# Moving the start of the first output projection's weight work on GpSimd ahead, into the last attention head

## The reference, cut to what matters

```
s = einsum('bqhd,bkhd->bhqk', qb, k) * scale;  s = where(causal, s, -inf)
pr = softmax(s);  out = einsum('bhqk,bkhd->bqhd', pr, v)
ym = mla_branch(...) * silu(gm)
mix = concatenate([ys, ym], axis=-1) @ w_out[i]
u = DEEPNORM_ALPHA * x + mix
ple = sigmoid(u @ w_pg[i]) * (p[i] @ w_pp[i])
```

```
ada = silu(c) @ w_ada[i] + b_ada[i]
```

## Time and profile before

| | |
|---|---|
| time, median of 3 runs | 2152.24 us (2151.87 to 2154.48) |
| the profiled execution's own time | 2153.62 us |
| its span in the profile | 2151.8 us |
| PE busy | 2074.0 us (96% of the span) |
| POOL busy | 1140.8 us (53%) |
| chain that ended last | PE 80%, DVE 8%, POOL 3%, ACT 3% |
| mean granted TensorE clock | 0.989 of full speed |

### The profile page before, as it was taken

One profiled execution on the slowest core, in us unless ns is written; L12 is line 12 of the kernel. 1 busy time (PEld: TensorE's weight loads), 2 busy tenths in 40 slices (PEclk: granted clock), 3 DMA queues, 4 the chain that ended last, 5 costly groups with the idle time before them and its releaser, 6 DMA issues.

```text
span 2151.8 us, 28447 instructions
## 1 busy us (share of the span) xinstructions
PE 2074.0 (96%) x11124; PEld 1629.0 (76%) x11124; DVE 1359.5 (63%) x1705; ACT 817.9 (38%) x1304; POOL 1140.8 (53%) x793
## 2 busy tenths in 40 slices
PE   8999999989998999999999999998999999999997
PEld 5878746978866885578757788876788888877885
DVE  7999865631967115510168325775977777778988
ACT  6232243330126006610174443145554554453443
POOL 2576713067872754337656664474787777850000
PEclk9999999999999999999999999999999999999998
DMA  7463461052224120101221235233122222247543
GB/s 302 146 144 108 115 173 63 1 205 92 89 90 140 60 98 28 28 30 69 57 48 56 82 118 205 88 118 137 50 80 73 83 89 88 69 159 256 186 139 112
DMA packets 72725, 230.02 MB, mean 107 GB/s; under 512 B 15959, under 2 KB 18823, under 8 KB 71279
## 3 DMA queue, kind: packets, MB, share of 16 engines
q1 hardware_dynamic: 59632, 170.04, 23.3%
q10 hardware_dynamic: 9104, 36.45, 4.6%
q0 software_dynamic: 3856, 21.70, 3.9%
HBM read 180.03 MB, written 46.17 MB: 105 GB/s over the span
## 4 chain that ended last, share of the span: by engine, by line
PE 80%; DVE 8%; POOL 3%; ACT 3%; issue 2%; DMA 2%; SPq 1%; ACTq 0%; DVEq 0%; POOLq 0%
PE ps L3563 22%; PE ps L3160 18%; PE ps L3678 8%; PE ps L3487 4%; PE ps L3596 4%; PE ps L3182 3%; PE ps L3634 2%; DVE back L2350 2%; PE ps L355 2%; PE ps L3125 1%; PE ps L525 1%; PE ps L513 1%; PE ps L378 1%; PE ps L507 1%; PE ps L538 1%
## 5 line engine op out<-in xcount | busy, mean ns | idle before, releaser
L1779 POOL TENSOR_TENSOR up_parts<-front,up_parts 128x512 fp32r<-128x512 f32 x120 | 188.6, 1581 | 74.6 <-ACT up_parts L2087 73.9
L3678 PE MATMUL ps<-ffn_parts,w_parts 128*128 128x512 f32 x924 | 214.5, 394 | 5.5 <-DVE ffn_parts L2946 5.4
L3678 PEld LDWEIGHTS ps<-ffn_parts,w_parts 128*128 128x128 f32 x924 | 175.3, 190 | 44.1 <-DVE w_parts L2938 3.8
L3563 PE MATMUL ps<-t_high,up_parts 128*128 128x512 f32 x640 | 204.1, 390 | 1.0 <-ACT back L2094 0.8
L3160 PE MATMUL ps<-h_high,w_parts 128*128 128x512 f32 x672 | 187.6, 394 | 0.6 <-PE ps L3487 0.6
L1704 POOL TENSOR_TENSOR w_parts<-front,sb_zero 128x1024 fp32r<-128x1024 f32 x48 | 100.4, 2091 | 161.9 <-PE ps L3487 61.7
L3563 PE MATMUL ps<-h_high,up_parts 128*128 128x512 f32 x480 | 154.9, 389 | 0.3 <-DVE back L2755 0.2
L1709 POOL TENSOR_TENSOR w_parts<-front,w_parts 128x1024 fp32r<-128x1024 f32 x54 | 142.9, 2647 | 19.3 <-ACT w_parts L2252 6.3
L3160 PEld LDWEIGHTS ps<-h_high,w_parts 128*128 128x128 f32 x672 | 124.0, 188 | 25.8 <-issue 1.4
L3563 PEld LDWEIGHTS ps<-t_high,up_parts 128*128 128x128 f32 x640 | 120.1, 188 | 27.1 <-issue 1.4
L1590 POOL TENSOR_TENSOR front<-front,sb_csilu 128x1024 f32<-128x1024 f32 x48 | 102.9, 2144 | 58.8 <-DMA front<-w_ada 58.7
(11 more groups left out here) (445 smaller groups left out, 5029.2 us busy)
## 6 DMA issues: line engine op xcount, KB each, us to landing
front<-w_ada SPq DMA_DIRECT2D x48, 512.0 KB, 3.5
front<-w_up SPq DMA_DIRECT2D x44, 512.0 KB, 4.2
front<-w_down SPq DMA_DIRECT2D x22, 512.0 KB, 3.6
back<-w_down SPq DMA_DIRECT2D x22, 512.0 KB, 4.4
front<-w_in SPq DMA_DIRECT2D x16, 512.0 KB, 4.2
front<-w_out SPq DMA_DIRECT2D x16, 512.0 KB, 4.4
residual<-back ACTq DMA_DIRECT2D x2, 4096.0 KB, 14.7
front<-w_gates SPq DMA_DIRECT2D x16, 512.0 KB, 4.3
```

The costliest lines, as they stand in the source:

```text
L1779: pool.tensor_tensor(parts[:, BANK:], src, parts[:, 0:BANK].bitcast(F32), ALU.subtract)\
L3563: mm = pe.matmul(o, parts[:, at + k * P:at + (k + 1) * P], x, start=p in (1, 2, 5) and k == 0 and q == 0, stop=k == 3 and q == 2, skip_gro ...
L3678: mm = pe.matmul(ps[:, (4 if p in (2, 5, 3) else 0) + m, :], weights[:, w_ * BANK + m * P:w_ * BANK + (m + 1) * P], half_of(x, x_), start= ...
```

## The change

GpSimd makes part of its work for the output projection earlier in its program: the parts of output block 0, modulation sum 16, the rounded part of block 1, and modulation sum 17 now stand ahead of the load of `XN`, behind a wait for the scores of the last head's first query block (`mla_scores_read` of 27: 25 score tiles and 2 turned heads). The low part of block 1 follows behind the load of `XN`. The loop over the blocks starts at 2, and the load of `PP`, which was issued behind block 0's parts, is issued behind block 2's.

```diff
+            def first_high(j):
+                b = B_WOUT + 2 * j
+                pool.wait_ge(S(f"w_landed{b % RING}"), 16 * (b // RING + 1))
+                pool.tensor_tensor(w_parts_1(b)[0], ring[:, b % RING, :], zero[:, 0:1].to_broadcast((P, PAGE)), ALU.add)\
+                    .then_inc(S("w_high"), 1)
+            def first_low(j):
+                b = B_WOUT + 2 * j
+                pool.wait_ge(S("w_high"), j + 1)
+                pool.tensor_tensor(w_parts_1(b)[1], ring[:, b % RING, :], w_parts_1(b)[0].bitcast(F32), ALU.subtract)\
+                    .then_inc(S("w_split"), 1)
+            pool.wait_ge(S("mla_scores_read"), 8 * (MLA_HEADS - 1) + MLA_HEADS - 1)
+            first_high(0)
+            first_low(0)
+            ada_sum(16)
+            first_high(1)
+            ada_sum(17)
             pool.wait_ge(S("mla_turned"), 32)
             pool.dma_start(XN, xn_dram).then_inc(S("xn_back"), 16)
...
-            for j in range(8):
+            first_low(1)
+            for j in range(2, 8):
                 split(B_WOUT + 2 * j)
-                if j == 0:
+                if j == 2:
                     pool.dma_start(PP, pp_dram.rearrange("a p k t -> p a k t")).then_inc(S("pp_back"), 16)
                 ada_sum(16 + j)
```

## The result

The changed kernel takes 2156.7 us in the median of 22 runs (2152.9 to 2163.5), the kernel before 2153.5 in 22; the ratio is 1.0017 with an interval of 1.0011 to 1.0024. It is slower by 0.17%, 3.7 us (2.4 to 5.2), where 2.2 less was forecast. One run of the kernel before took 2603 us and is not part of the comparison. The profiled execution took 2154.1 us with a span of 2152.3.

What follows compares the result with a forecast made beforehand. PE, busy for 96% of the span, was taken to bound the kernel, so only its waits could be won: -4.2 for earlier products + 2.0 for a new stall = -2.2, and 2152.24 - 2.2 = 2150.0 us, range 2147.8 to 2152.9.

Steps and rivals of the forecast that it cites:

- The two waits: PE's waits for GpSimd's low parts ahead of products 0 and 1 of the output projection, 3.7 us together, would go.
- the gain: Products 0 and 1 start earlier without their waits: 1.86, 2.19 and 0.11 us, sum 4.2, at least 3.7.
- GpSimd's work did not slow the last head: Moved GpSimd work beside the attention's last head priced at nothing; the slower rival said 2159.1 us, chance 0.04.
- the 1.3 us kept for them: Possible loss in product 0 if DVE's four low parts took 2.06 us each; not priced, kept for the range.
- the new wait: PE waits ahead of product 3 for GpSimd's low part, held up by modulation block 18's load, about 2 us.
- The allowed 7.5 us: Time modulation block 18's load may take before product 3 is late; every microsecond more stalls PE.
- that is about 9.5 and a stall of 2.0: Modulation block 18's load beside PP's takes about 9.5 us, so PE stalls 2.0 ahead of product 3.
- about 1 for queueing: Part of the time of modulation block 18's load: about 1 us for queueing behind packets already taken.
- the 85 used: Rate in GB/s of SP's queue beside PP's load, giving 6.2 us for modulation block 18's 0.52 MB.
- The row of 12.0: Output block 2's load beside XN and PP took 12.0 us, not 3.5; used as upper case, stall 4.5.
- the sum of rates: Duration of modulation block 18's load: 6.2 us at 85 GB/s, 2.4 for start and landing, about 1 for queueing.
- The meeting costs the whole: Rival: modulation block 18's load takes 12.0 us or more beside PP's, stall 4.5, time 2152.5 to 2153.9; chance 0.15.

Runs made afterwards that it cites:

- the repeat: The changed kernel run once more, unedited, timed against the kernel before: ratio 1.0011 (1.0002 to 1.0020).
- the first experiments: Follow-up runs timed beside the kernel before, not listed singly; the first one told moved PP's load right behind XN's in the changed kernel: ratio 0.9974.
- the run from ScalarE's queue: The changed kernel with PP's load issued from ScalarE's queue behind the sixth bias piece, at 462.80 us: ratio 1.0016 (1.0007 to 1.0025) to the kernel before.
- the kernel before with the collision: The kernel before, nothing made ahead, with PP's load moved to just ahead of block 2's parts: ratio 1.003 (1.002 to 1.0039).

## Why the prediction was wrong

**Right.** The two waits went, and the gain was 4.2 to 4.3: SP's issue of block 18 came 21.86 behind the turning before (467.95 - 446.09) and 17.58 after (463.28 - 445.70). GpSimd's work did not slow the last head: 640-wide tiles read 23.99 apart there (416.13 to 440.12), as between the heads before (392.14 to 416.13). DVE's four low parts took 4.63 instead of the 8.24 of the earlier trace rows, 1.16 each instead of 2.06, while GpSimd stood idle (446.4 to 458.1); so the 1.3 us kept for them were not needed, and XN's chain was in time. The place of the new wait, its cause, PP's issue (462.4 where 462.6 was forecast) and the load's (463.3 where 463.65 was) came out as written. The allowed 7.5 us were right too: 12.1 - 7.5 = 4.6, measured 4.4.

**Wrong, first: the duration of the load in PP's company.** The wait ahead of product 3 was 4.4, where the prediction had about 2 and called itself wrong above 4. The step "that is about 9.5 and a stall of 2.0" is the one that failed, and in it the "about 1 for queueing". In the changed kernel SP's queue moved its first packets between 467.2 and 467.4, about 4 us behind the issue at 463.28, where alone (the load at 467.95 in the kernel before) it had them about 1 us behind; so the start costs some 3 more, not 1. By 474 the queue had moved 0.52 MB, in 6.8 us at 77 GB/s, near the 85 used and the 6.2 that came of them. So 2 of the missing 2.6 us are the start and 0.6 the rate. The late start stood already in the trace of the kernel before: the load that took 12.0 was issued at 448.79, and SP's queue is absent from the view of 450 to 452 us (first row) and has 16 packets in that of 452 to 454 (second row), over 3 us behind the issue:

```profile
q0 software_dynamic: 24, 0.79, 91.0%
...
q1 hardware_dynamic: 16, 0.07, 8.0%
```

The row of 12.0 was the better guide than the sum of rates: it was set aside because XN's packets are larger, and that made no difference to the total. "The meeting costs the whole" was the rival that came true.

**Wrong, second: a term that no case had.** The prediction looked for the price of a stall only in PE's waiting. Behind a stall of 4.4 us the clock stood at half for 3.5 us, and half a product took 1.8 us longer. With it the sum is -4.3 + 4.4 + 1.8 = +1.9, and the trace has nearly that, 2.0: the column of product 3 ended 44.08 behind the turning before (490.17 - 446.09), and 46.11 after (491.81 - 445.70). The same 2.0 still stands in later products (616.53 - 446.09 before, 618.17 - 445.70 after), and half of it goes in the norm that follows (653.29 - 446.09 before, 653.88 - 445.70 after), where the granted clock was 0.81 over 630 to 665 us against 0.76; the span ends 0.5 longer. That the clock made this difference is likely, not shown.

**Open.** The 22 runs say 3.7 (2.4 to 5.2), the repeat 2.4 (0.4 to 4.3), the trace 2.0. The mean granted clock over the 22 runs was 0.9880, in 33 runs of the kernel before (those beside the first experiments) 0.9894, so the changed kernel seems to spend more time at half clock than its profiled executions show. The 8.24 of the run from ScalarE's queue, where the other traces have 7.3 to 7.4, is one way in which that can come about. How often it does, no trace shows.

The range ended at 2152.9, since it held the rival's cost without what follows a stall. With both terms the sum would be -4.2 + 4.5 + 1.8 = +2.1, still a little under the 2.4 at which the interval of the 22 runs begins. And 1.2 of the distance from 2150.0 to 2156.7 is the starting point: the kernel before has a median of 2153.5 in 22 runs, and had 2152.24 in the three that the forecast went by.

## What to carry to other kernels

When work is made earlier, list every DMA issue that moves with it, and see which small load that the critical engine depends on is issued within the next microseconds: a load of 4 MB with 16 KB packets turned one of 0.5 MB from 3.5 into 12 us. Put the large one where the small ones have slack, or cut it so that its packets are as short. Price a stall of TensorE of some 4 us above its length, for the clock behind it (here 1.8 to 2.7 more, restart included); and where the trace has one row of the disputed wait, take it before a figure built from rates. Here the early start is worth 0.26% (0.16 to 0.36) with PP's load moved up, and was -0.17% without.

## What the runs showed that was not expected

- Two queues on the same DMA engines got equal numbers of packets, not of bytes: 41 to 39 with 0.67 to 0.16 MB, and 114 to 116 with 0.43 to 0.41 MB. The Trainium skill ("DMA: Bandwidth & Descriptors", section "Queues, rings and completion order") has this rule, and the trace agrees, if the packets of the profile are taken as those of the Trainium skill; the same from SP and ScalarE (38 to 40) as from SP and GpSimd.
- A load issued behind another starts late: first packets about 4 us behind the issue with 16 KB packets ahead and 3 with 4 KB packets, against about 1 alone. That was 2 of the 2.6 us misjudged.
- A DMA issue on ScalarE's queue went out at 455.93, with the first of six instructions of 1.05 us each that stood in front of it; only a wait on their semaphore put it at 462.80.
- The granted clock fell to half with 4.0 to 4.4 us without a matmul, in all four traces that have such a stall in the products (the changed kernel twice, the kernel before with the collision, PP from ScalarE's queue at 462.8), and did not fall behind the 2.0 of the kernel before. Half a product then took 7.32, 7.34, 7.36 and 8.24 where the pace is 5.5.
